# Stick-breaking attention on one core: sums of later key blocks and their low parts on GpSimd, and new instruction lists for the last pair of heads

## What is computed

```python
z = einsum('bqhd,bkhd->bhqk', q, k) * HD_B ** -0.5 + bias
mask = arange(Lk)[None, :] < (q_offset + arange(Lq))[:, None]
u = where(mask, log_sigmoid(-z), 0.0)
rev_excl = cumsum(u, axis=3, reverse=True) - u
A = where(mask, exp(log_sigmoid(z) + rev_excl), 0.0)
out = einsum('bhqk,bkhd->bqhd', A, v)
```

## Time and profile before

| what | value |
|---|---|
| median of 3 runs | 1500.58 us (1500.52 to 1502.69) |
| the profiled execution, its own time | 1502.18 us |
| span of its trace | 1500.4 us |
| PE, DVE, ACT, POOL busy | 98%, 79%, 55%, 22% of the span |
| mean granted PE clock | 0.999 |

### The profile page before, as it was taken

How to read it: one execution, slowest core, us unless ns; L and a number is a source line. 1 busy time by engine, 2 the same in 40 slices (tenths; PEclk the granted TensorE clock), 3 DMA queues, 4 the chain that set the end, 5 groups by cost and what they waited for, 6 DMA issues and landing times.

```text
span 1500.4 us, 33609 instructions
## 1 busy us (share of the span) xinstructions
PE 1476.8 (98%) x12928; PEld 1397.7 (93%) x12928; DVE 1181.6 (79%) x2014; ACT 827.7 (55%) x1312; POOL 333.6 (22%) x330
## 2 busy tenths in 40 slices
PE   8999999999999999999999999999999999999998
PEld 8999999989999999999998888887699999999998
DVE  7866666667898988989834888888789989898753
ACT  6554444435664645546533777777756546364543
POOL 3000000002332232232142122112233332232221
PEclk9999999999999999999999999999999999999999
DMA  6233333223777877777425555543338777778621
GB/s 191 58 87 88 87 87 87 87 87 87 139 170 157 179 164 161 176 153 155 135 85 176 186 191 197 184 156 114 100 86 168 177 159 168 166 157 187 142 85 64
DMA packets 237716, 205.83 MB, mean 137 GB/s; under 512 B 8268, under 2 KB 224404, under 8 KB 237588
## 3 DMA queue, kind: packets, MB, share of 16 engines
q1 hardware_dynamic: 151346, 147.34, 31.6%
q0 software_dynamic: 68160, 47.20, 20.4%
q10 hardware_dynamic: 18082, 9.48, 2.3%
HBM read 192.19 MB, written 11.80 MB: 136 GB/s over the span
## 4 chain that ended last, share of the span: by engine, by line
PE 94%; DVE 2%; ACT 2%; issue 1%; DMA 0%; DVEq 0%; ACTq 0%
PE acc L2904 23%; PE acc L3227 18%; PE pL L3227 12%; PE pM L3227 9%; PE acc L3327 6%; PE pO L3227 3%; PE acc L3165 2%; PE pL L3025 1%; PE pL L3368 1%; PE pO L3401 1%; PE pM L3382 1%; PE acc L3444 1%; PE acc L3461 1%; PE pM L3094 1%; PE pM L3388 1%
## 5 line engine op out<-in xcount | busy, mean ns | idle before, releaser
L658 POOL TENSOR_TENSOR wlo<-wraw,whi 128x512 fp32r<-128x512 f32 x40 | 56.2, 1435 | 449.3 <-ACT whi L795 449.3
L2904 PE MATMUL acc<-xa_hi,whi 128*128 128x288 f32 x544 | 125.0, 311 | 0.2 <-DVE hT L2355 0.2
L881 ACT ACTIVATE hi<-wraw 128x1024 fp32r<-128x1024 f32 x60 | 63.7, 1061 | 104.2 <-DVE wraw L2025 104.2
L864 ACT ACTIVATE hi<-wraw 128x1024 fp32r<-128x1024 f32 x60 | 63.7, 1061 | 103.0 <-PE acc L3227 102.8
L2904 PE MATMUL acc<-xa_hi,wlo 128*128 128x288 f32 x544 | 116.5, 296 | 0.0
L2904 PE MATMUL acc<-xa_lo,whi 128*128 128x288 f32 x544 | 116.1, 295 | 0.0
L3227 PE MATMUL acc<-X_lo,hi 128*128 128x288 f32 x384 | 113.3, 295 | 0.0
L3227 PE MATMUL acc<-X_hi,lo 128*128 128x288 f32 x384 | 113.3, 295 | 0.0
L3227 PE MATMUL acc<-X_hi,hi 128*128 128x288 f32 x384 | 113.1, 294 | 0.0
L2040 DVE TENSOR_TENSOR lo<-wraw,hi 128x1024 fp32r<-128x1024 f32 x60 | 73.3, 1222 | 42.4 <-ACT hi L864 42.4
L3227 PE MATMUL acc<-H_hi,hi 128*128 128x288 f32 x336 | 99.3, 296 | 1.3 <-DVE lo L2046 1.3
(11 more groups left out here) (549 smaller groups left out, 5135.2 us busy)
## 6 DMA issues: line engine op xcount, KB each, us to landing
wraw<-in_w_up_dram SPq DMA_DIRECT2D x64, 512.0 KB, 6.4
wraw<-in_w_down_dram SPq DMA_DIRECT2D x64, 512.0 KB, 5.5
Kp<-in_cache_k_dram SPq DMA_DIRECT2D x32, 512.0 KB, 4.4
Vp<-in_cache_v_dram SPq DMA_DIRECT2D x32, 512.0 KB, 5.4
wraw<-in_w_in_a_dram SPq DMA_DIRECT2D x30, 512.0 KB, 5.6
wraw<-in_w_up_dram POOLq DMA_DIRECT2D x32, 256.0 KB, 4.8
S_even<-in_w_up_dram POOLq DMA_DIRECT2D x32, 256.0 KB, 6.3
S_odd<-in_w_up_dram POOLq DMA_DIRECT2D x32, 256.0 KB, 6.9
```

The lines of the kernel that those rows point to most:

```text
L658: ins = pool.tensor_tensor(wlo[s][:, k:k + 2, :], wraw[s][:, k:k + 2, :], whi[s][:, k:k + 2, :].bitcast(F32), ALU.subtract)
L864: act.activation(blocks4(hi02), by_rows(G % 2)[:, 0], ACT.Copy).then_inc(piece_hi, 1)
L881: act.activation(blocks4(hi31), by_depth(G % 2)[:, 0], ACT.Copy).then_inc(piece_hi, 1)
L2904: last = pe.matmul(acc[a][:, hf, 0:HALF], w[s][:, k, a * P:(a + 1) * P], x[k][:, hf * HALF:(hf + 1) * HALF], start=(k == 0 and n == 0), st ...
```

## The change

Both sums of later blocks are now made ahead on GpSimd, each with its low part, and group 2 needs one product of the ones matrix per part instead of two. `later_sum_0` adds block 1's columns of queries 256 to 511 and the sum of blocks 2 and 3; ACT rounds it into `uh[:, 512:768]` once `later_sums` of n = 2 + hh has read what was there. `kv_low` is issued in halves. The last pair's lists are reordered on PE, ACT and DVE, and its `new_values` moves behind the last `later_sums`. Counts of the semaphores `bias_ready`, `u_hi` and `u_lo` follow. The diff, cut:

```diff
 POOL
             def later_sum_1(j, hh):
-                pool.wait_ge(u_lo, N_U * j + U_AT[hh])
+                pool.wait_ge(u_lo, 6 * j + hh + 1)
...
+            def later_low_1(j, hh):
+                pool.wait_ge(u_hi, high_count(j, "s1", hh))
+                pool.tensor_tensor(ul[hh][:, S1_COLS], tl[hh][:, S1_COLS], uh[hh][:, S1_COLS].bitcast(F32), ALU.subtract
+                                   ).then_inc(bias_ready, 1)
+            def later_sum_0(j, hh):
+                pool.wait_ge(u_lo, 6 * j + hh + 3)
+                pool.wait_ge(bias_ready, pool_count(j, "a1", hh))
+                pool.tensor_tensor(tl[2 + hh][:, P:3 * P], tl[2 + hh][:, P:3 * P], tl[hh][:, P:3 * P], ALU.add
+                                   ).then_inc(bias_ready, 1)
+            def later_low_0(j, hh):
+                pool.wait_ge(u_hi, high_count(j, "s0", hh))
+                pool.tensor_tensor(ul[hh][:, S0_COLS], tl[2 + hh][:, P:3 * P], uh[hh][:, S0_COLS].bitcast(F32), ALU.subtract
+                                   ).then_inc(bias_ready, 1)
             def turn_sums(j):
                 later_sum_1(j, 0)
-                kv_low(j + 2, 0)
+                kv_low_half(j + 2, 0, 0)
                 later_sum_1(j, 1)
+                later_low_1(j, 0)
+                kv_low_half(j + 2, 0, 1)
                 masked_bias(j + 1)
+                later_sum_0(j, 0)
+                later_low_1(j, 1)
+                later_sum_0(j, 1)
+                later_low_0(j, 0)
+                later_low_0(j, 1)
...
 ACT
+            def later_high_0(j, hh):
+                act.wait_ge(bias_ready, pool_count(j, "a0", hh))
+                act.wait_ge(R_full, 7 * j + hh + 4)
+                act.activation(uh[hh][:, S0_COLS], tl[2 + hh][:, P:3 * P], ACT.Copy).then_inc(u_hi, 1)
 pair
                 u_high(j, 4)
+                later_high_0(j, 0)
                 weights(j, 0)
                 weights(j, 1)
                 weights(j, 2)
                 u_high(j, 5)
+                later_high_0(j, 1)
 last_pair, from softplus(j, 3) on
                 softplus(j, 3)
+                u_high(j, 2)
+                later_high_1(j, 0)
                 softplus(j, 4)
-                u_high(j, 2)
                 u_high(j, 3)
-                later_high_1(j, 0)
+                later_high_1(j, 1)
+                u_high(j, 4)
+                later_high_0(j, 0)
                 softplus(j, 5)
-                later_high_1(j, 1)
+                later_high_0(j, 1)
+                ob_high(NB - 2)
                 weights(j, 0)
-                u_high(j, 4)
+                u_high(j, 5)
                 new_factor(j)
                 new_weights(j)
-                u_high(j, 5)
                 weights(j, 1)
-                ob_high(NB - 2)
 DVE, pair
                 logits_in(j, 5)
-                later_low_1(j, 0)
                 t_copy(j + 1, 7)
...
                 sp_add(j, 4)
-                later_low_1(j, 1)
                 minus_later(j, 2)
 DVE, last_pair: the new list from new_sp on
+                new_sp(j); logits_in(j, 2); logits_in(j, 3); sp_add(j, 0); past_store(j); sp_add(j, 1); u_low(j, 0)
+                logits_in(j, 4); ob_low(3); sp_add(j, 2); minus_later(j, 0); u_low(j, 1); logits_in(j, 5); ob_low(4)
+                u_low(j, 2); minus_later(j, 1); sp_add(j, 3); sp_add(j, 4); minus_later(j, 2); u_low(j, 3)
+                attn_out(j - 1); u_low(j, 4); ob_low(5); minus_later(j, 3); new_sub(j); sp_add(j, 5); ob_low(6)
+                minus_later(j, 4); u_low(j, 5); new_out(j)
 PE
+                if g:
+                    pe.wait_ge(bias_ready, pool_count(j, ("l1", "l0")[g - 1], hh))
-                later = [(LATER[g], GW[g])] if g < 2 else [(LATER[2], GW[2]), (LATER[1], GW[2])]
+                later = [(LATER[g], GW[g])]
 last_pair, after ob_prompt_part(1, 2)
-                ob_prompt_part(0, 3)
                 later_sums(j, 0)
                 new_sums(j)
+                ob_prompt_part(0, 3)
                 later_sums(j, 1)
                 ob_prompt_part(1, 3)
                 ob_prompt_part(0, 4)
                 later_sums(j, 2)
                 ob_prompt_part(1, 4)
                 later_sums(j, 3)
+                ob_prompt_part(0, 5)
+                later_sums(j, 4)
+                ob_prompt_part(1, 5)
+                later_sums(j, 5)
                 new_values(j)
-                later_sums(j, 4)
-                ob_prompt_part(0, 5)
-                later_sums(j, 5)
-                ob_prompt_part(1, 5)
                 ob_prompt_part(0, 6)
```

More of the change, by code:

```diff
@@ L175, in yoco_step @@
         LATER = [slice(0, 128), slice(128, 384), slice(384, 768)]
[L176 to L179, removed]
+        S1_COLS, S0_COLS = slice(256, 384), slice(512, 768)
+        HIGH_AT = [{"u": (1, 2, 3, 4, 7, 9), "s1": (5, 6), "s0": (8, 10)},
+                   {"u": (1, 2, 3, 5, 7, 10), "s1": (4, 6), "s0": (8, 9)}]
+        POOL_AT = [{"a1": (1, 2), "l1": (3, 6), "a0": (5, 7), "l0": (8, 9)},
+                   {"a1": (1, 2), "l1": (3, 5), "a0": (4, 6), "l0": (7, 8)}]
         qT_at = (limit - NB * T * 4) // 64 * 64
@@ L446, in yoco_step, with last_turn, high_count, pool_count @@
         tok2 = "p (a b) -> p a b"
+        def last_turn(j):
+            return isinstance(j, int) and j == NPAIR - 1
+        def high_count(j, what, n):
+            return 10 * j + HIGH_AT[last_turn(j)][what][n]
+        def pool_count(j, what, hh):
+            return 9 * j + 1 + POOL_AT[last_turn(j)][what][hh]
         def accv(a):
@@ L752, in later_sum_1, with kv_low_half @@
             def later_sum_1(j, hh):
-                pool.wait_ge(u_lo, N_U * j + U_AT[hh])
+                pool.wait_ge(u_lo, 6 * j + hh + 1)
                 pool.tensor_tensor(tl[hh][:, S1_COLS], tl[hh][:, S1_COLS], tl[hh][:, 0:P], ALU.add).then_inc(bias_ready, 1)
+            def later_low_1(j, hh):
[11 more added lines that the diff above has]
+                                   ).then_inc(bias_ready, 1)
+            def kv_low_half(j, a, q):
+                cols = slice(a * P, (a + 1) * P)
+                if q == 0:
+                    pool.wait_ge(kv_hi, 2 * j + a + 1)
+                ins = pool.tensor_tensor(wlo0[:, 4 * q:4 * q + 4, cols], wraw0[:, 4 * q:4 * q + 4, cols],
+                                         whi0[:, 4 * q:4 * q + 4, cols].bitcast(F32), ALU.subtract)
+                if q:
+                    ins.then_inc(kv_lo, 1)
             def turn_sums(j):
                 later_sum_1(j, 0)
-                kv_low(j + 2, 0)
+                kv_low_half(j + 2, 0, 0)
                 later_sum_1(j, 1)
+                later_low_1(j, 0)
+                kv_low_half(j + 2, 0, 1)
                 masked_bias(j + 1)
+                later_sum_0(j, 0)
[3 more added lines that the diff above has]
+                later_low_0(j, 1)
             kv_low(0, 0)
@@ L776, in _ @@
             later_sum_1(NPAIR - 1, 1)
+            later_low_1(NPAIR - 1, 0)
+            later_sum_0(NPAIR - 1, 0)
+            later_low_1(NPAIR - 1, 1)
+            later_sum_0(NPAIR - 1, 1)
+            later_low_0(NPAIR - 1, 0)
+            later_low_0(NPAIR - 1, 1)
             pool.wait_ge(lo_done, U_OB // 2 + 1)
@@ L2585, in logits_in @@
                 if g == 0:
-                    dve.wait_ge(bias_ready, 1 if isinstance(j, int) and j == 0 else 3 * j - -1)
+                    dve.wait_ge(bias_ready, 1 if isinstance(j, int) and j == 0 else 9 * j - 4)
                 nd = len(GROUPS[g])
@@ L2605, in u_low @@
                 cols = slice(GCOL[g], GCOL[g] + GW[g])
-                dve.wait_ge(u_hi, N_U * j + H_AT[n])
+                dve.wait_ge(u_hi, high_count(j, "u", n))
                 dve.wait_ge(sp_done, 6 * j + n + 1)
                 dve.tensor_tensor(ul[hh][:, cols], tl[n][:, 0:GW[g]], uh[hh][:, cols].bitcast(F32), ALU.subtract
[L2609 to L2614, removed]
                                   ).then_inc(u_lo, 1)
@@ L2753, in last_pair @@
                 new_sp(j)
-                ob_low(3)
-                sp_add(j, 0)
                 logits_in(j, 2)
                 logits_in(j, 3)
+                sp_add(j, 0)
+                past_store(j)
                 sp_add(j, 1)
-                attn_out(j - 1)
-                past_store(j)
+                u_low(j, 0)
                 logits_in(j, 4)
-                u_low(j, 0)
+                ob_low(3)
+                sp_add(j, 2)
+                minus_later(j, 0)
                 u_low(j, 1)
                 logits_in(j, 5)
-                minus_later(j, 0)
-                sp_add(j, 2)
+                ob_low(4)
+                u_low(j, 2)
+                minus_later(j, 1)
                 sp_add(j, 3)
[L2768 to L2771, removed]
+                sp_add(j, 4)
+                minus_later(j, 2)
                 u_low(j, 3)
-                sp_add(j, 4)
-                later_low_1(j, 1)
+                attn_out(j - 1)
+                u_low(j, 4)
+                ob_low(5)
```

(11 more changed lines are left out.)

3 lines of the change are left out of this document (1 added, 2 removed).

## The result

The changed kernel takes **1508.89 us** (median of 6 runs, 1507.79 to 1511.45), the kernel before 1500.88 (6 runs, 1500.34 to 1502.69). The ratio is 1.0055, with a 95% interval of 1.0042 to 1.0068. The forecast was 1498.9 with a range up to 1501.3: the change made the kernel slower, on the side to which the forecast gave a chance of 0.06.

The account below looks back on a forecast made before the run. PE, busy 98% of the span, was taken as the bound. Seven turns gaining 2.4 us and the last pair losing 0.7 gave -1.7 us, 1498.9 us against the median 1500.58; range 1496.2 to 1501.3.

Parts of the forecast that it names:

- What the steps on GpSimd do to VectorE: In each turn, overlap costs VectorE 0.13 us per GpSimd step: six steps 0.8 us against 0.69 it loses, neutral.
- VectorE steps twice as long beside GpSimd: A sign, listed for the profile after, that would show the forecast wrong.
- The lock's rival: VectorE stands still while GpSimd works: 1.8 us a turn, 2.7 in the last pair, +13 in all, 1513.5; chance 0.05.
- GpSimd's prices: Steps added per turn on GpSimd: 0.46 us for 128 columns, 0.61 for 256, together 3.4 us on an idle engine.
- The products: Seven turns: PE sheds 0.46 us of products for n = 4 and 5, 0.34 kept per turn, 2.4 us gained.
- The last pair: The four new lists lose 0.7 us, as weighted waits behind new_values and new_out; bounds -0.5 to +1.5.
- What I called covered: In the turns, ScalarE's two added copies, GpSimd's longer queue and SP's later weight load cost nothing, hidden by idle time.

Follow-up runs that it names:

- e1: The changed kernel with all waits and lists, but the moved GpSimd steps work on 2 columns instead of 128 or 256; 1500.53 us, ratio 0.9993.
- e7: Turns 0 to 6 as in the kernel before, last pair as changed but with new_values ahead of later_sums(j, 5); 1503.36 us, ratio 1.0014.
- e9: As e7, with ScalarE's split of the next weight panel moved behind weights(j, 5); 1505.10 us, ratio 1.0025.
- e4: The changed kernel with all four low parts of a turn made on VectorE, the sums staying on GpSimd; 1509.89 us, ratio 1.0060.
- e8: The changed turns with GpSimd's steps placed beside VectorE's PSUM reads, later_low_0(j, 0) on VectorE, last pair as before; 1502.29 us, ratio 1.0003.
- e6: The changed kernel with only later_low_0 cut to 2 columns; 1502.46 us, ratio 1.0003.
- e11: The turns of e8; last pair in e9's order, but with two products and later_low_1 on VectorE; 1504.31 us, ratio 1.0018.

## Why the prediction was wrong

**The step that failed** is "What the steps on GpSimd do to VectorE". I took the 0.41 against 0.28 us of one `later_low_1` as a rate, 0.13 us lost per step, and called six steps neutral. It was not a rate but a remainder. GpSimd's step beside it, from the trace of before:

```profile
935.29 0.46 POOL L755 TENSOR_TENSOR tl<-tl 128x128 f32<-128x128 f32 x1
```

It was over at 935.75, and VectorE's instruction had begun at 935.49. Taken as "stands until the step is over", the same row gives the lock. The loss is then up to a whole step, and depends on when the two meet. The trace after shows 0.55 us for `u_low(4)` and 0.36 for the zbS subtraction, as well as 0.28 for the `u_low` at 938.97 and 0.09 for the `sp_add` at 940.78. Counted from `keys_transposed`, the zbS subtraction ends 1.06 us later than before (0.70 in its start, 0.36 of its own), and PE waits 0.78 at the transposes. "VectorE steps twice as long beside GpSimd" stood among the forecast's own signs of being wrong, and `u_low(4)` nearly is.

**The lock's rival** was the right mechanism, with chance 0.05, at about twice its true price. It let VectorE stand for all of GpSimd's time and came to 1.8 us a turn and 2.7 in the last pair. By e1, the lock costs (240.42 - 233.18) / 7 = 1.03 us a turn and 26.62 - 25.27 = 1.35 in the last pair. It was less because VectorE is held only in instructions with both inputs in SBUF, while GpSimd's steps also fall beside PSUM reads and gaps, or wait themselves, as for the scan. The two rules of the Trainium skill that the prediction weighed are contention with VectorE's instructions of two SBUF inputs (GPSIMD Engine Reference, Specifications) and an exclusive lock (Trainium Architecture — The Big Picture, What this means for kernel authors). This trace agrees: an instruction with two SBUF inputs is held, 0.68 to 1.23 us, one with an input in PSUM is not, 0.54 and 0.54.

**GpSimd's prices.** I priced 256 columns at 0.61, from `masked_bias`. The new steps took 0.73 us at the least, and 1.08 us in the median for `later_low_0`, which also has waits for VectorE inside. It mattered through the lock alone; PE never waited for GpSimd.

**The products** were right in size. Without the lock (e1) a turn takes 33.05 us against 33.32, 0.27 less where I had 0.34 and bounds of 0.23 to 0.46: -2.1 us in all instead of -2.4.

**The last pair** was right in its walk: +0.7 forecast, +0.5 in e1. The bounds ended at +1.5 because I allowed 0.13 us a step for the lock; with it the measured loss is +1.84. In the trace after, PE waits 1.58 ahead of `ob_prompt_part(0, 5)` (I had 1.1), 0.78 ahead of n = 5 (0.8), 1.31 ahead of `weighted` (1.3), and VectorE idles 1.45 ahead of `new_out` (1.7). The excess of the first is the lock again:

```profile
1072.86 1.21 DVE L2796 TENSOR_TENSOR xb_lo<-qT,xb_hi 128x512 fp32r<-128x512 f32 x1
1073.68 0.98 POOL L785 TENSOR_TENSOR ul<-tl,uh 128x256 fp32r<-128x256 f32 x1 [0.16 <-ACT uh L1498]
1074.12 0.50 PE L3578 MATMUL acc<-xb_hi,whi 128*128 128x512 f32 x1 [1.58 <-DVE xb_lo L2796]
```

The order costs 0.5 us (e1), the rest, 1.35, is the steps on GpSimd. The cause that I named, `new_values` behind n = 5, is worth 0.5 us when undone (e7); ScalarE's panel split, which I had not named, 0.9 more (e9).

**What I called covered.** The copies on ScalarE, the queue on GpSimd and SP's load were covered, as no new wait of PE names them. VectorE's time ahead of `past_later` was not: 0.9 us of idle that I counted as cover lies partly behind it, which e4 and e8 show from two sides.

## What to carry to other kernels

Work moved to an idle GpSimd is not free while VectorE runs instructions with both inputs in SBUF: look for what each step will meet, and charge the whole remaining step to it, if that instruction leads to the bounding engine. A single row with a small loss shows how long the overlap was, not what an overlap costs: line up the ends of both instructions before you use it. Where such steps must go to GpSimd, put them beside VectorE's reads of PSUM, and when a split on another engine is moved, look at what GpSimd will then start and when.

## What the runs showed of the hardware that was not expected

- The exclusion works in both directions. GpSimd's subtraction of 256 columns took 0.73 us where it was placed beside a PSUM read (e8) and 1.41 when it met VectorE's scan, ending 0.53 us after it.
- The scan, begun just before such a step, was not lengthened itself (1.21 us). One that began while a step was running took 1.33 (e8).
- A GpSimd step that met nothing took 0.20 us for 2 columns, 0.46 for 128, 0.73 for 256 and 1.27 for 512: by these rows 0.2 us and about 0.21 for each 100 columns. What it costs VectorE depends on the columns too: with 2 of them `u_low` kept its 0.68 us.
- In two of the fourteen profiled executions (e6, e11) the clock granted to TensorE fell to 0.54 for 3.75 us in the last pair. It cost 0.9 us each time, half of what the last pair lost by the change, so two such stretches can be compared only with the granted clock of each beside them.
- Ten steps of 128 columns per turn (10 x 0.46 = 4.6 us of GpSimd's time when nothing holds them) that nobody needs made the kernel 7.3 us longer, about 1.2 us a turn.

Not tried: whether GpSimd steps with a single SBUF input hold VectorE as well, and what the other steps of the last pair cost one by one.
